# Attention block: division by the row sums moved behind P V, output rows transposed by TensorE, output bias added by DVE

## The reference

```python
qb = q.reshape(B, nb, ATTN_BLOCK, ATTN_KV_HEADS, ATTN_GROUP, ATTN_HEAD_DIM)
scores = einsum('bnqhgd,bnkhd->bnhgqk', qb, kb) * (ATTN_HEAD_DIM ** -0.5)
scores = where(valid, scores, -inf)            # window of 128 keys
m = maximum(max(scores, -1), sink)
p = exp(scores - m)
probs = p / (sum(p, -1) + exp(sink - m))       # learned sink per head
o = einsum('bnhgqk,bnkhd->bnqhgd', probs, vb).reshape(B, S, ATTN_Q_W)
return o @ w_out + b_out
```

## Time and profile before

| | before |
|---|---|
| median of 3 runs | 1062.3 us |
| lowest, highest | 1061.82, 1063.28 us |
| profiled execution | 1062.27 us |
| its span | 1060.5 us |
| TensorE busy | 1037.3 us (98%) |
| DVE busy | 602.9 us (57%) |
| ACT busy | 533.6 us (50%) |
| POOL busy | 68.0 us (6%) |

### The profile page before, as it was taken

The page is one execution under the profiler, slowest core; times in us unless marked ns, Lnnn a source line. Parts: engine busy times, 40 slices in busy tenths (PEclk is TensorE's granted clock), DMA queues, the critical chain, the costliest instruction groups (busy, mean ns, idle before and its releaser), DMA issues.

```text
span 1060.5 us, 14343 instructions
## 1 busy us (share of the span) xinstructions
PE 1037.3 (98%) x5304; PEld 872.5 (82%) x5304; DVE 602.9 (57%) x824; ACT 533.6 (50%) x808; POOL 68.0 (6%) x143
## 2 busy tenths in 40 slices
PE   9999999987999999999999999899999999999997
PEld 7888888864788888888888888799999988888886
DVE  5645454568655454545645554567587566455543
ACT  7444353555563443535444353477567545443532
POOL 0000000153000000000000000502202200000000
PEclk9999999999999999999999999999999999999999
DMA  9754555441156555553664555423143146555521
GB/s 326 235 195 159 213 220 179 155 155 41 55 177 217 186 164 214 215 184 112 219 199 158 208 216 184 141 91 120 41 160 114 47 159 221 195 160 211 215 87 40
DMA packets 123694, 174.67 MB, mean 165 GB/s; under 512 B 7280, under 2 KB 97664, under 8 KB 123648
## 3 DMA queue, kind: packets, MB, share of 16 engines
q1 hardware_dynamic: 120976, 171.73, 47.3%
q10 hardware_dynamic: 2672, 2.32, 0.7%
HBM read 172.98 MB, written 1.05 MB: 164 GB/s over the span
## 4 chain that ended last, share of the span: by engine, by line
PE 92%; DVE 4%; ACT 2%; POOL 1%; issue 1%; ACTq 0%; POOLq 0%; DVEq 0%
PE bank L1434 27%; PE bank L1436 27%; PE bank L1435 27%; PE bank L1738 2%; PE bank L1508 2%; PE bank L1732 2%; PE bank L1709 1%; PE bank L1465 1%; DVE prob L1217 1%; ACT w_hi L664 1%; PE bank L1648 0%; DVE w_lo L1022 0%; PE bank L1832 0%; DVE sm_max L1203 0%; DVE x_sb L1043 0%
## 5 line engine op out<-in xcount | busy, mean ns | idle before, releaser
L1022 DVE TENSOR_TENSOR w_lo<-w_raw,w_hi 128x2048 fp32r<-128x2048 f32 x159 | 362.0, 2295 | 150.5 <-ACT w_hi L664 150.5
L664 ACT ACTIVATE w_hi<-w_raw 128x2048 fp32r<-128x2048 f32 x159 | 301.5, 1918 | 114.5 <-PE bank L1436 114.0
L1434 PE MATMUL bank<-w_hi,xT_hi 128*128 128x512 f32 x784 | 310.1, 396 | 1.0 <-DVE w_lo L1149 0.7
L1436 PE MATMUL bank<-w_hi,xT_lo 128*128 128x512 f32 x784 | 305.7, 390 | 0.0
L1435 PE MATMUL bank<-w_lo,xT_hi 128*128 128x512 f32 x784 | 305.2, 389 | 0.0
L1434 PEld LDWEIGHTS bank<-w_hi,xT_hi 128*128 128x128 f32 x784 | 147.2, 188 | 32.9 <-issue 2.2
L1436 PEld LDWEIGHTS bank<-w_hi,xT_lo 128*128 128x128 f32 x784 | 147.1, 188 | 30.9
L1435 PEld LDWEIGHTS bank<-w_lo,xT_hi 128*128 128x128 f32 x784 | 147.4, 188 | 29.6 <-issue 0.2
L706 ACT ACTIVATE silu_g<-bank,rstd 128x256 f32<-128x256 f32 x88 | 37.0, 472 | 247.0 <-PE bank L1436 246.9
L1434 PE MATMUL bank<-w_hi,hT_hi 128*128 128x512 f32 x352 | 138.0, 392 | 0.0
L1436 PE MATMUL bank<-w_hi,hT_lo 128*128 128x512 f32 x352 | 137.1, 389 | 0.0
(11 more groups left out here) (287 smaller groups left out, 977.5 us busy)
## 6 DMA issues: line engine op xcount, KB each, us to landing
w_raw<-in_ffn_w_gate_up SPq DMA_DIRECT2D x170, 512.0 KB, 4.6
w_raw<-in_ffn_w_down SPq DMA_DIRECT2D x88, 512.0 KB, 4.1
w_raw<-in_gdn_w_in SPq DMA_DIRECT2D x32, 512.0 KB, 4.4
w_raw<-in_attn_w_in SPq DMA_DIRECT2D x12, 512.0 KB, 4.1
w_raw<-in_attn_w_out SPq DMA_DIRECT2D x8, 512.0 KB, 4.1
w_raw<-in_gdn_w_out SPq DMA_DIRECT2D x8, 512.0 KB, 3.9
w_raw<-in_ffn_w_gate_up SPq DMA_DIRECT2D x12, 256.0 KB, 5.6
x_sb<-in_x SPq DMA_DIRECT2D x4, 256.0 KB, 5.2
```

What stands on the lines that cost most here:

```text
L664: act.activation(w_hi[u0 % RING][:], w_raw[u0 % RING][:], ACT.Copy).then_inc(hi_ready, 1)
L1022: dve.tensor_tensor(w_lo[u0 % RING][:], w_raw[u0 % RING][:], w_hi[u0 % RING][:].bitcast(F32), ALU.subtract).then_inc(split_ready, 1)
L1434: pe.matmul(out_ap, a[0], b[0], start=start, stop=False, **kw)
L1436: return pe.matmul(out_ap, a[1], b[0], start=False, stop=stop, **kw)
```

## The change

The probabilities stay unscaled. TensorE makes P V with the transposed probabilities stationary and V (64 columns, no padding) moving, so that the result has query rows on the partitions. DVE multiplies these rows by the reciprocals of the sums, one instruction for 8 heads (512 columns) out of PSUM into `y_sb`, and TensorE transposes them back into the same bank (`o_transposes_att`). The sink's argument, its exponential, the sum and the reciprocal are made for four items at once. ACT copies out of the bank one step later than before (`OUT_STEP` = 8, 12, 16, 20). The output bias is added by DVE in four pieces of 512 columns at steps 10 to 13, and POOL no longer does it. The padded V, its memsets and its copies go. The output products inside the loop begin at step 14 and not 12; there are eight as before.

```diff
-OUT_FIRST, OUT_PARTS = 12, [1] * 6 + [2]
+OUT_FIRST, OUT_PARTS = 14, [1, 1, 2, 2, 2]
...
-OUT_STEP = [i + 4 for i in OUT_LAST]
+OFF_STEP = OUT_LAST
+SINK_STEP = [i + 1 for i in OUT_LAST]
+INV_STEP = [i + 2 for i in OUT_LAST]
+ROW_STEP = [i + 4 for i in OUT_LAST]
+OUT_STEP = [i + 5 for i in OUT_LAST]
+BIAS_STEP = 10
...
-            v_pad = [sb(f"v_pad{t}", [P, HKV, 2, P], F32, att_mem) for t in range(TT)]
+            v_rows = [sb(f"v_rows{t}", [P, HKV, DH], F32, att_mem) for t in range(TT)]
...
-                pool.memset(k_pad[t][:], 0.0)
-                z = pool.memset(v_pad[t][:], 0.0)
+                z = pool.memset(k_pad[t][:], 0.0)
...
-                pool.wait_ge(v_row, t + 1)
-                pool.tensor_copy(v_pad[t][:, :, 1, DH:P], v_pad[t][:, :, 0, 0:DH]).then_inc(v_both, 1)
...
-                pool.tensor_tensor(x_sb[:, t, :], x_sb[:, t, :], b_out[:], ALU.add).then_inc(bias_added, 1)
...
-            for s in range(STEPS + 1):
+            for s in range(STEPS + 2):
...
-                    act.activation(sm_sink[:, s, :], sm_off[:, s, :], ACT.Exp).then_inc(exp_done, 1)
+                    z.then_inc(exp_done, 1)
+                for n in range(len(OUTS)):
+                    if s == SINK_STEP[n]:
+                        act.wait_ge(off_ready, n + 1)
+                        act.activation(sm_sink[:, 4 * n:4 * n + 4, :], sm_off[:, 4 * n:4 * n + 4, :],
+                                       ACT.Exp).then_inc(sink_done, 1)
...
-                        act.wait_ge(pv_done, OUT_PV[n])
+                        act.wait_ge(oT_psum, n + 1)
...
-                    for h in range(2):
-                        z = dve.tensor_scalar(prob[i % PROBS][:, h, 0:keys], prob[i % PROBS][:, h, 0:keys],
-                                              sm_inv[:, i, h:h + 1], None, ALU.mult)
-                    z.then_inc(prob_ready, 1)
+                for n, (c, t) in enumerate(OUTS):
+                    four = slice(4 * n, 4 * n + 4)
+                    if s == OFF_STEP[n]:
+                        dve.wait_ge(max_ready, s + 1)
+                        dve.tensor_tensor(sm_off[:, four, :], sm_nmax[:, four, :],
+                                          sink[:, 8 * c:8 * c + 8].rearrange("p (i h) -> p i h", h=2),
+                                          ALU.add).then_inc(off_ready, 1)
+                    if s == INV_STEP[n]:
+                        dve.wait_ge(exp_done, OUT_LAST[n] + 1)
+                        dve.wait_ge(sink_done, n + 1)
+                        after(dve.tensor_tensor(sm_total[:, four, :], sm_sum[:, four, :], sm_sink[:, four, :], ALU.add))
+                        after(dve.reciprocal(sm_inv[:, four, :], sm_total[:, four, :]))
+                    if s == ROW_STEP[n]:
+                        dve.wait_ge(pv_done, OUT_PV[n])
+                        dve.tensor_tensor(
+                            y_sb[:, t, c * BANK:(c + 1) * BANK].rearrange("p (h d) -> p h d", d=DH),
+                            bank[2 * c + t][:].rearrange("p (h d) -> p h d", d=DH),
+                            sm_inv[:, four, :].rearrange("p i h -> p (i h)").unsqueeze(2).broadcast_to([P, 8, DH]),
+                            ALU.mult).then_inc(o_row, 1)
+                if BIAS_STEP <= s < BIAS_STEP + 4:
+                    t, half = (s - BIAS_STEP) // 2, (s - BIAS_STEP) % 2
+                    at = slice(half * BANK, (half + 1) * BANK)
+                    dve.wait_ge(xT_psum, 4 * E_ATT + 4)
+                    dve.wait_ge(ssq_ready, TT * (E_ATT + 1))
+                    dve.tensor_tensor(x_sb[:, t, at], x_sb[:, t, at], b_out[:, at], ALU.add).then_inc(bias_added, 1)
...
+            def o_transposes_att(n):
+                c, t = OUTS[n]
+                pe.wait_ge(o_row, n + 1)
+                for m in range(4):
+                    z = pe.transpose(bank[2 * c + t][:, m * P:(m + 1) * P],
+                                     y_sb[:, t, c * BANK + m * P:c * BANK + (m + 1) * P], ident[:])
+                z.then_inc(oT_psum, 1)
...
-                        pe.wait_ge(prob_ready, items[-1] + 1)
+                        pe.wait_ge(exp_done, items[-1] + 1)
...
-                                z = pe.matmul(o, v_pad[b][:, p // 2, h, :], pT[:, m * P:(m + 1) * P],
-                                              start=(m == 0), stop=(m == 3))
+                        rows = bank[2 * (p // HALF_PAIRS) + t]
+                        for m in range(4):
+                            i, h, b = (m % 2, m // 2, 0) if t == 0 else (0, m // 2, m % 2)
+                            head = 2 * (p % HALF_PAIRS + i) + h
+                            z = pe.matmul(rows[:, head * DH:(head + 1) * DH], pT[:, m * P:(m + 1) * P],
+                                          v_rows[b][:, p // 2, :], start=(b == 0), stop=(b == t))
                         z.then_inc(pv_done, 1)
+                for n in range(len(OUTS) - 1):
+                    if s == ROW_STEP[n]:
+                        o_transposes_att(n)
...
             for d in range(OUT_UNITS):
+                if d == 1:
+                    o_transposes_att(len(OUTS) - 1)
```

More of the change, by code:

```diff
@@ L318, in build @@
         exp_done = sem("exp_done")
-        prob_ready = sem("prob_ready")
+        off_ready = sem("off_ready")
+        sink_done = sem("sink_done")
+        o_row = sem("o_row")
+        oT_psum = sem("oT_psum")
         pv_done = sem("pv_done")
@@ L578, in _ @@
                     pool.wait_ge(q_rot, 2 * c + t + 1)
-            pool.wait_ge(a_loaded, 16 * A_LOADS)
-            for t in range(TT):
-                pool.wait_ge(xT_psum, 4 * E_ATT + 4)
-                pool.wait_ge(ssq_ready, TT * (E_ATT + 1))
-                pool.tensor_tensor(x_sb[:, t, :], x_sb[:, t, :], b_out[:], ALU.add).then_inc(bias_added, 1)
             pool.wait_ge(unit_done, U_GDN)
@@ L810, in _ @@
                     for h in range(2):
-                        act.activation(pr[:, h, 0:keys], bank[6 + s % 2][:, h * keys:(h + 1) * keys], ACT.Exp,
-                                       scale=DH ** -0.5, bias=sm_nmax[:, s, h:h + 1], accum_out=sm_sum[:, s, h:h + 1])
-                    act.activation(sm_sink[:, s, :], sm_off[:, s, :], ACT.Exp).then_inc(exp_done, 1)
+                        z = act.activation(pr[:, h, 0:keys], bank[6 + s % 2][:, h * keys:(h + 1) * keys], ACT.Exp,
+                                           scale=DH ** -0.5, bias=sm_nmax[:, s, h:h + 1],
+                                           accum_out=sm_sum[:, s, h:h + 1])
+                    z.then_inc(exp_done, 1)
[4 more added lines that the diff above has]
+                                       ACT.Exp).then_inc(sink_done, 1)
                 for n, items in enumerate(FILLS):
@@ L1180, in _ @@
             for t in range(TT):
-                for dst, col, signal in ((k_pad, 0, k_row), (v_pad, HKV * DH, v_row)):
+                for dst, col, signal in ((k_pad[t][:, :, 0, 0:DH], 0, k_row), (v_rows[t][:], HKV * DH, v_row)):
                     dve.scalar_tensor_tensor(
-                        dst[t][:, :, 0, 0:DH], bank[ATT_BANKS[0][t]][:, col:col + HKV * DH].rearrange(
+                        dst, bank[ATT_BANKS[0][t]][:, col:col + HKV * DH].rearrange(
                             "p (h d) -> p h d", d=DH), rstd[:, t:t + 1],
@@ L1204, in _ @@
                         "p (h k) -> p h k", h=2), AX, ALU.max))
[L1205 to L1219 removed]
+                    dve.scalar_tensor_tensor(sm_nmax[:, s, :], sm_max[:, s, :], -DH ** -0.5,
+                                             nsink[:, 2 * p:2 * p + 2], ALU.mult, ALU.min).then_inc(max_ready, 1)
@@ L1634, in _ @@
             q_part(range(8, Q_FIRST))
-            pe.wait_ge(v_both, TT)
+            pe.wait_ge(v_row, TT)
             pe.wait_ge(a_mask, 1)
```

24 lines of the change are left out of this document (1 added, 23 removed).

## The result

| | before | after |
|---|---|---|
| median of 5 runs, us | 1062.3 (1061.8 to 1063.4) | 1066.5 (1064.5 to 1068.1) |
| profiled execution, us | 1062.27 | 1064.47 |
| its span, us | 1060.5 | 1062.7 |
| its mean granted TensorE clock | 0.999 | 0.995 |

The changed kernel takes 1.0038 times as long, with a 95% interval of 1.0022 to 1.0055: slower, by 4.2 us in the median. The profiled execution is its fastest one, so the traces show only 2.2 us of the 4.2.

A forecast was written before the change was run, and what follows sets the result against it. The prediction took TensorE, 92% of the span, as the bound. Five legs, -2.1 - 0.6 + 1.5 + 0.7 + 2.7 = +2.2 us, on the profiled 1062.27 (median 1062.3) gave 1064.5 us, range 1060.0 to 1066.6.

The forecast's parts named there:

- Leg A: Up to the first score: without POOL's V copies the 1.84 wait before the second q transposes goes; -2.1 us.
- P V with 64 columns: P V products in the attention block: weight load sets the pace, 0.9 us a group against 0.89, no gain.
- Leg B: Steps 0 to 7: waits for scaling go, new transposes cost 0.5, idle falls from 3.6 to 2.4; -0.6 us.
- Leg C: Steps 8 to 11: DVE waits for a_oT_hi ahead of maximum 9, TensorE 3.4 before P V; +1.5 us.
- Leg D: Steps 12 to 18: same ACT-DVE handshake at step 12, 2.0 us idle on TensorE; +0.7 us.
- Leg E: Output units: transposes 0.5, and TensorE stalls 2.2 before the third unit until w_lo is made; +2.7 us.
- rival 2: POOL's last q rotation starts after DVE's split and is still held, the 1.84 stays: 1066.4 us; chance 0.13.
- Rival 1: DVE's wait at steps 8 and 12 does not reach TensorE, 3.4 and 2.0 go: 1059.1 us; chance 0.18.
- rival 3: Narrow P V passes are cheap, a group at 0.5, 2.9 us arrives: 1061.6 us; chance 0.12.

The follow-up runs named there:

- x4_filler: Changed kernel with 24 unread transposes of the identity in TensorE's idle piece before P V of item 7; median 1064.4 us, ratio to before 1.0014.
- p3: Changed kernel with POOL's two copies of V put back, into a tile nothing reads; median 1069.3 us, ratio to before 1.0059.
- x1: Changed kernel with DVE making a_oT_lo one step later, behind the next item's maximum; median 1062.4 us, ratio to before 0.9992.
- x7: x3 with the second output unit's weight split one step later on ACT and two on DVE; median 1056.1 us, ratio to before 0.9947.
- x3: Changed kernel with the edits of x1 and x2 together; median 1061.0 us, ratio to before 0.9983.
- x5: Changed kernel with ACT's weight split put behind a_oT_hi in step 8; median 1063.5 us, ratio to before 1.0007.
- x2: Changed kernel with the third output unit split before a_oT_hi and a_oT_lo of the last tile; median 1064.4 us, ratio to before 1.0012.
- p2: Changed kernel with POOL adding the whole output bias again in place of DVE's four pieces; median 1068.2 us, ratio to before 1.0047.
- x10: x3 with 16 unread transposes of the identity in the idle piece before P V of item 7; median 1059.4 us, ratio to before 0.9971.

## Why the prediction was right, and where its steps were off

It said slower as the likeliest side, 1064.5, up to 1066.6. The time is 1066.5: at the very end of the range. The path came out 1 us shorter than I had it at full clock, and the clock, which no step had, put about 3 us on top. That the time is still inside the range is luck. The traces allow each leg to be laid beside its measurement, in the execution whose clock fell and at full clock (x4_filler):

| leg | predicted | after, profiled | x4_filler |
|---|---|---|---|
| A, to the first score | -2.1 | -2.7 | -2.1 |
| B, to score 8 | -0.6 | -1.0 | -1.0 |
| C, to score 12 | +1.5 | +1.5 | +1.1 |
| D, to the first output unit | +0.7 | +1.5 | +0.4 |
| E, to the third | +2.7 | +2.7 | +2.7 |
| sum | +2.2 | +2.0 | +1.1 |

The spans differ by 2.2 and 1.3, so about 0.2 lies outside the legs.

**Leg A was right.** The 1.84 before the second q transposes is gone, the last rotation takes 0.33, p3 brings both back. The 2.7 instead of 2.1 is in part the first loads: the first scores of the variants that leave this part alone start anywhere between 228.7 and 229.4.

**P V with 64 columns was right.** Eight passes take 0.84 (246.61 to 247.45), 0.105 apart, where I took 0.9; half the columns brought 0.05 a group. The row of 16-column passes was the right neighbour. By the Trainium skill, TensorE: Matmul & The Clock Gate, section LDWEIGHTS, a load of 128 columns takes an estimated 107 ns (columns / 1.2), which the 0.105 bears out. The 60 cycles of its section Back-to-back issue gap, which stand there for a matmul by itself without the load, do not show here.

**Leg B** gained 0.4 more than I had; its two named pieces are there, 0.57 at step 6 and 1.54 before the q transposes of step 7 (I had 0.6 and 1.5). Where the 0.4 lies is left open. The list of idle pieces in the prediction's first paragraph left out two of before in leg C, 1.38 (at 259.23, ended by ACT's probT) and 0.86 (at 261.80); the sum does not suffer, since it takes the 10.70 as measured.

**Leg C had the right mechanism and was mis-sized by 0.4.** DVE waits 3.75 for a_oT_hi (predicted 3.9), TensorE 3.22 (3.4). Of the 3.22 the turn over DVE is 1.4 (x1) and the split of 1.92 in ACT's row the rest (x7). The piece before the transposes of step 11 was 1.51 at full clock and not 1.8, and score 12 comes 11.8 behind score 8 and not 12.2. In after it comes at 12.21, only because the clock had fallen: the agreement of the profiled number with mine is two errors that cancel.

**Leg D** was over-sized by 0.3 at full clock (its idle piece was 1.81 and not 2.0). Its 1.5 in after holds about 1.1 of low clock.

**Leg E was right**: 2.05 in front of the third output unit, ended by w_lo, and 0.5 of transposes.

**What no step of mine had is the clock.** I priced the idle piece of 3.2 us by its length. All twelve executions of the changed kernel have a lower mean clock (0.993 to 0.997) than the usual 0.998 to 0.999 of before. At full clock the change costs 1.1 to 1.3 us by the path, less than the 2.1 that the prediction took for the least that can be measured; in the median it costs 4.2. The difference of about 3 us is the clock's. The executions of x4 at 0.999 say the same of the structure: 1062.8 to 1063.5 against 1061.7 to 1062.4 of before at that clock in the same group, 1.0 to 1.5 more, and 3.1 less than the changed kernel's 1066.4 in the median. Shown for the clock: the 1.2 GHz stretch behind the piece in the windows, its absence in x4 with the same waits and more work, and that time follows clock over the executions of one kernel. x1's 4.0 us in the median is only in part this effect: 2.65 of it is the path, at two steps (x3's trace), and its three executions at 0.998 or more, 1060.2 to 1060.4, lie about 3 under those of x4 at 0.999. By this the sum would have been right about the structure and wrong about the time, had I not left the range open upward for another reason (rival 2).

**The rivals.** Rival 1 (the handshake is covered) is wrong as the change stands, but x1 and x5 show how near it was. x3 and x7 with it and the last stall taken out are at 1061.0 and 1056.1. Rival 2 is wrong by leg A, rival 3 by the 0.105.

**What stays open** is what decides over each fall. Read in windows of 0.5 us, the fourteen traces of this case have 17 falls ahead of the last few us. Each begins within about 1.5 us of TensorE starting again behind an idle piece of 1.5 to 3.2 us and lasts 3.5 to 7.5 us, wherever in the kernel it is: behind the 3.22 in after, behind pieces of about 1.5 in x2, x5 and p2 (at 247, where after has such a piece too and keeps 1.00), and in x2, x3 and x10 behind one of 1.9 in the other mixer (near 676 to 681), where no edit reaches and where before has 1.94 and no fall. In the attention block all five pieces of 2.7 us or more were followed by a fall, and 9 of the 34 between 1.5 and 2.1. So the long piece makes a fall near certain in these traces, a shorter one makes it possible, and what tells the shorter ones apart is not known. Before has executions at 0.994 to 0.997 too (1062.3 to 1065.5), without a piece of 3 us. Whether one fall makes the next more likely was not tested.

## What to carry to other kernels

When a step is moved, look at what stands behind its wait on each in-order engine: here one subtraction that waited for ACT held the next maximum, and with it one step later and two weight splits put elsewhere, the same change is 6 us faster than the kernel before and not 4 slower (no run has such moves in the kernel before, so the 6 us are not the change's alone). An idle piece of 3 us on an otherwise full TensorE costs more than its length, so read the granted clock right behind it, over several executions, before trusting a sum made from one. And taking a hold off an engine is worth only what the next waiter lets through: 4 us of it off DVE, with 2.8 us of bias pieces in its place, gave 0.5 us in the trace and nothing measurable in the median.
